# Mixture-of-experts stage of a fused decoder layer: routing inside the output projection, experts ordered by their token count, tokens held stationary

## The chip, the cores and the metric

One core of one Trainium2 chip runs the whole layer as one program. The metric is the device time of one execution in microseconds; the kernel before takes 1448.4 us (median of 3 runs, 1447.89 to 1451.6). All data are float32.

Five engines run their own instruction streams and meet at semaphores: TensorE (PE; its weight loads are shown as PEld), VectorE (DVE), ScalarE (ACT), GpSimd (POOL) and SyncE (SP). SP issues direct transfers on one queue, POOL issues direct and indirect (gather and scatter) transfers on another. 16 DMA engines serve both.

## The reference, cut to what matters

1056 tokens (1024 of a prompt, 32 of decoding) of 1024 features go through one layer: token mixers, an output projection `w_out` with a residual, a mixture of experts, and a gated embedding at the end. The mixture is what the change is about:

```
m        = rms_norm(h, g_ffn)                                # 1056 x 1024
g_sel    = argmax of m @ w_router_group                      # 1 of 4 groups
top_i    = top 2 of (m @ w_router_expert) in that group      # 2 of its 8 experts
w_k      = softmax(top 2 values) * softmax(group logits)[g_sel]
for each of the token's two experts e (32 experts in all):
    hidden = silu(m @ w_gate[e]) * (m @ w_up[e])             # 1024 -> 256, twice
    out   += w_k * (hidden @ w_down[e])                      # 256 -> 1024
h        = h + out
```

Each expert has 3 MB of weights, 32 experts 100.7 MB. There are 2112 (token, expert) pairs, 66 an expert on average. Worked out with the reference on its own inputs, the counts of the 32 experts run from 32 to 122. Experts 0 to 3 have 88, 60, 55 and 73 tokens. The other 28 sorted are 122, 111, 106, 89, 85, 83, 78, 75, 74, 74, 71, 67, 63, 61, 60, 59, 57, 56, 55, 53, 51, 47, 46, 45, 43, 37, 36, 32.

## The kernel before, in words

The program is written engine by engine (raw streams, no scheduler); the order of the code in each engine's block is the order on the engine, and each PE, ACT, DVE or DMA step counts up a semaphore that others wait for. Only the stages from the output projection on matter here.

*Output projection* (from `step_e` on each engine). For each of 9 tiles of 128 tokens (the last has 32), PE multiplies the attention half and the convolution half by `w_out` (`out_part`, L1710, for the last tile L1700). Between them it transposes the normalised row `m` of the tile before (`router`, L1726), and after them computes that tile's 36 router logits (`logits`, L1737). DVE adds the residual (L1209, L1215), makes `m` (`make_m`, L1226) and copies the logits (`take_logits`, L1232). POOL stores `m` to `m_dram` (L626). SP loads expert 0's weights before this stage.

*Routing* (DVE from L1265, PE L1760 and L1761, POOL L640 and L644). After the last logits DVE works out for all 9 tiles at once the group, the two experts, each token's rank within its expert (two matmuls with a matrix of ones and a triangular one give counts and ranks), and overflow blocks for experts with more than `CAP` = 128 tokens. POOL then writes each token's number into `list_dram` with 18 indirect transfers (2 choices x 9 tiles) and reads the lists back. SP loads experts 1 to 3 meanwhile.

*Experts* (`turn`, `block_act`, `take_rows`, `hidden`, `gather`, `scatter`). One block is one expert with up to 128 tokens; 32 blocks in the experts' own order. For a block POOL gathers up to 128 rows of `m_dram` into `xg` (L657), PE transposes them (`trans_rows`, L1769), DVE copies them out (L1357). PE multiplies with the gate and up weights as the stationary operand and 128 tokens as the moving one (`up`, L1778), which leaves `hidden` already transposed. ACT applies silu (L894), DVE multiplies (L1363). PE multiplies with `w_down` (`down`, L1788), ACT copies the result out (L898, L900) and POOL scatters the rows to `y_dram` (L669). PE's order in a steady block is `up(n)`, `trans_rows(n+1)`, `down(n-1)`. The weights sit in 4 slots; SP loads expert n+4 after `down(n)` (L491 to L493). 16 overflow blocks follow under an `If`.

*End*. SP loads `w_ple_gate`, `w_ple_proj` and the rows of `y_dram`; the two expert results are combined and the gated embedding is computed.

The lines that set the order in a steady block of PE and of POOL are these:

```
up(n, s % 2, s, i)
if not final:
    trans_rows(n + 1, 1 - s % 2, 2 * i + (s + 1) // 2)
if not begin:
    down(n - 1, 1 - s % 2, (s - 1) % 4)
...
gather(2 * i + 4 + u, u)
scatter(2 * i + u, u, i)
```

Of the kernel before, what the change touches and what calls it, by code (L numbers as in the profile page):

```python
# [80 lines left out]
def constants():  # L81
# [39 lines left out]
    c["c_blk"] = np.tile(np.arange(NOV, dtype=np.float32)[None, :], (P, 1))  # L121
# [33 lines left out]
KV_DONE = (32, 32, 0, 0, 0)  # L155

# [32 lines left out]
def _build(nc, I, O, ctx):  # L189
# [14 lines left out]
    list_dram = nc.dram_tensor("list_dram", [CAP * NBLK, 2], I32).ap()  # L204
# [16 lines left out]
    misc = sb("misc", 64)  # L221
# [67 lines left out]
    m_st = [view(R1, 12576 + 1024 * s, D) for s in range(2)]  # L289
    mT = [view(R1, 14624 + 1024 * s, DC, P) for s in range(2)]  # L290
    junkE = R1[:, 19744:19744 + 512].bitcast(BF16)
    h = view(R1, 0, TILES, D)

    scratch_at = [21504]

    def scratch(*dims):
        at = scratch_at[0]
        scratch_at[0] += int(np.prod(dims))
        assert scratch_at[0] <= 26880
        return view(R1, at, *dims)  # L300

    r_ms, r_h1, r_h2, r_t, r_tot, r_rank, r_a = (scratch(T, NE) for _ in range(7))
    r_cum = scratch(T + 1, NE)
    r_big = scratch(NE, NTH - 1)
    r_ov = scratch(4, NE)
    r_bb = scratch(NOV, NE)
    r_be = scratch(NOV)
    r_hg, r_hg2, r_ge = (scratch(T, GROUPS) for _ in range(3))
    r_c10 = scratch(T, NTH - 1)
    r_mg, r_ig, r_m1, r_i1, r_m2, r_i2, r_rk, r_bs, r_c, r_s, r_z, r_x, r_gw, r_e2 = (scratch(T) for _ in range(14))  # L310
    pos_i = sb("pos_i", 2 * TILES, I32)
    code = sb("code", 4 * TILES, I32)
    blk = sb("blk", NOV)
    ov_e = sb("ov_e", NOV, I32)
    small_i = sb("small_i", 4, I32)
    lg = sb("lg", TILES * RG)[:, :].rearrange("p (t c) -> p t c", t=TILES)

    SLOTS = [R4[:, 0:6144], R2[:, 0:6144], R1[:, 9216:15360], R1[:, 15360:21504]]
    wg = [s[:, 0:2048].rearrange("p (c f) -> p c f", c=DC) for s in SLOTS]
    wu = [s[:, 2048:4096].rearrange("p (c f) -> p c f", c=DC) for s in SLOTS]  # L320
# [51 lines left out]
    def _(sp):  # L372
# [27 lines left out]
        sp.dma_start(blk[:, :], I["c_blk"]).then_inc(S("code_in"), 16)  # L400
        sp.wait_ge(S("relbd_zero"), 1)
# [100 lines left out]
        load_expert(0, 0)  # L502
        over_tiles(sp, lambda prev, cur, nxt: load_x2(nxt) if nxt is not None else None)


        sp.wait_ge(S("logits_done"), TILES)
        sp.wait_ge(S("out0"), 32 * USES[0])
        sp.wait_ge(S("out1"), 32 * USES[1])
        for s in range(1, 4):
            load_expert(s, s)  # L510
        with sp.Fori(0, NE // 4 - 1) as i:
            for s in range(4):
                sp.wait_ge(S("y_full"), 8 * i + 2 * s + 2)
                load_expert(4 * i + 4 + s, s)
# [5 lines left out]
        sp.wait_ge(S("y_full"), 2 * NE)  # L520
        over = sp.value_load(small_i[0:1, 0:1], min_val=0, max_val=NOV)
        with sp.If(over > 0):
            for s in range(4):
                load_expert(sp.value_load(ov_e[0:1, s:s + 1], min_val=0, max_val=NE - 1), s)
            with sp.Fori(1, NOV // 4) as i:
                for s in range(4):
                    sp.wait_ge(S("y_full"), 2 * NE + 8 * i + 2 * s - 6)
                    load_expert(sp.value_load(ov_e[0:1, bass.ds(4 * i + s, 1)], min_val=0, max_val=NE - 1), s)
# [1391 lines left out]
```

## Time and profile before

| | |
|---|---|
| median of 3 runs | 1448.4 us |
| the profiled execution: its own time / span | 1454.46 / 1452.4 us |
| mean granted TensorE clock | 0.931 of full speed |
| PE / DVE / ACT / POOL busy | 87 / 28 / 22 / 12 % of the span |
| chain that ended last | PE 81 %, DMA 6 %, DVE 6 % |
| output projection (PE's first matmul to the last logits) | 675 to 818.6 us |
| routing (last logits to the first `up`) | 818.6 to 880.3 us |
| experts (first `up` to the end of the last `down`) | 880.3 to 1263.1 us |
| end | 1263.1 to 1452.4 us |

Durations below are of the profiled execution, 6.1 us above the median. A fully busy PE in a window does not say how fast it is, since matmuls overlap: a float32 matmul is two instructions, and the time from one group of them to the next is what counts. The four stage borders are from the timeline and from the chain of waits.

### The profile page before, as it was taken

The page shows a single profiled execution, that of the slowest core. Times are in us where ns is not written, and L with a number is a line of the kernel's source. Part 1 is how long each engine was busy: PE and PEld are TensorE (multiplying, and loading weights), DVE is VectorE, ACT ScalarE, POOL GpSimd, SP SyncE. Part 2 cuts the span into 40 slices and gives each one's busy share as a digit, 9 for nine tenths or more (in the row PEclk, how much of TensorE's full clock was granted, in tenths as well). Part 3 has the DMA queues.
Part 4 walks back from the last instruction along what each step waited for, and adds up shares of the span by engine and source line. Part 5 has one row for each costly group of instructions (what it writes and reads, how often), then busy time and mean ns, then how long its engine had stood idle before and what let it go on. Part 6 is the DMA issues. An engine that isn't in the chain of part 4 may idle for free.

```text
span 1452.4 us, 16889 instructions
## 1 busy us (share of the span) xinstructions
PE 1262.4 (87%) x6484; PEld 816.4 (56%) x6484; DVE 403.7 (28%) x829; ACT 320.8 (22%) x625; POOL 168.5 (12%) x222
## 2 busy tenths in 40 slices
PE   4999999999978887567999407999999999789995
PEld 1444445666555557243555307888888888534442
DVE  1121221122257775121322531111111111033332
ACT  2132321000057664130111200111111111123332
POOL 0000000000031221000000052222222221100000
PEclk9999999999979998787999758999999999979998
DMA  7111400130040005898111422888888888432210
GB/s 260 36 51 43 119 15 19 44 102 0 27 127 31 30 1 162 202 267 301 73 73 47 191 89 64 308 308 294 310 297 322 317 318 327 189 129 90 86 50 33
DMA packets 64453, 208.84 MB, mean 144 GB/s; under 512 B 16158, under 2 KB 29758, under 8 KB 48528
## 3 DMA queue, kind: packets, MB, share of 16 engines
q1 hardware_dynamic: 50704, 177.61, 35.6%
q0 software_dynamic: 13696, 30.49, 5.8%
q8 instruction: 37, 0.61, 0.2%
q14 instruction: 16, 0.13, 0.0%
HBM read 194.43 MB, written 29.89 MB: 154 GB/s over the span
## 4 chain that ended last, share of the span: by engine, by line
PE 81%; DMA 6%; DVE 6%; issue 3%; ACT 2%; POOL 1%; SPq 1%; POOLq 0%; ACTq 0%; DVEq 0%
PE pair L1778 17%; PE pair L1473 12%; PE pair L1525 11%; PE pair L1710 8%; PE pair L1877 8%; PE pair L1788 8%; DMA R<-in_cache_v 4%; PE pair L1552 3%; PE pair L1566 2%; PE pair L1769 2%; PE pair L1859 2%; PE pair L1579 2%; DVE R L1101 1%; PE pair L1603 1%; POOL list_dram L640 1%
## 5 line engine op out<-in xcount | busy, mean ns | idle before, releaser
L1778 PEld LDWEIGHTS pair<-R 128*128 128x128 f32 x2048 | 247.6, 197 | 16.5 <-issue 14.2
L1778 PE MATMUL pair<-R 128*128 128x128 f32 x2048 | 247.9, 282 | 1.7 <-DVE R L1357 1.7
L1525 PE MATMUL pair<-R 128*128 128x352 f32 x576 | 172.5, 463 | 0.4 <-ACT kts L758 0.4
L1473 PE MATMUL pair<-R 128*128 128x512 f32 x384 | 170.6, 601 | 0.8 <-DVE R L993 0.8
L1525 PEld LDWEIGHTS pair<-R 128*128 128x128 f32 x576 | 110.2, 192 | 61.8 <-issue 1.4
L1473 PEld LDWEIGHTS pair<-R 128*128 128x128 f32 x384 | 72.9, 193 | 87.8 <-issue 86.6
L1788 PE MATMUL pair<-R,bias_s 128*128 128x512 f32 x256 | 115.3, 593 | 1.4 <-DVE bias_s L1363 1.4
L1710 PE MATMUL pair<-R 128*128 128x512 f32 x256 | 114.6, 602 | 0.0
L1877 PE MATMUL pair<-R 128*128 128x512 f32 x256 | 112.9, 599 | 0.8 <-ACT R L932 0.8
L1357 DVE COPY R<-pair 128x512 f32<-128x512 f32 x64 | 41.3, 686 | 238.2 <-PE pair L1769 238.2
L1877 PEld LDWEIGHTS pair<-R 128*128 128x128 f32 x256 | 49.2, 193 | 62.9 <-issue 62.9
L898 ACT ACTIVATE R<-pair 128x512 f32<-128x512 f32 x32 | 19.1, 597 | 292.4 <-PE pair L1788 292.4
L1710 PEld LDWEIGHTS pair<-R 128*128 128x128 f32 x256 | 48.3, 193 | 55.6 <-issue 55.6
L1769 PE MATMUL pair<-ident,R 128*128 128x128 f32 x256 | 34.3, 278 | 45.8 <-DMA R<-m_dram,idx_c 45.8
L1788 PEld LDWEIGHTS pair<-R,bias_s 128*128 128x128 f32 x256 | 46.2, 190 | 48.2 <-issue 45.9
L1566 PE MATMUL pair<-ident,R 128*128 128x128 f32 x288 | 46.3, 302 | 22.1 <-DVE R L1101 16.2
L1769 PEld LDWEIGHTS pair<-ident,R 128*128 128x128 f32 x256 | 31.5, 189 | 46.6 <-issue 46.6
L1566 PEld LDWEIGHTS pair<-ident,R 128*128 128x128 f32 x288 | 34.0, 151 | 40.6 <-DVE R L1101 36.2
L807 ACT ACTIVATE R<-pair 128x512 f32<-128x512 f32 (+3 forms) x96 | 43.8, 484 | 43.3 <-PE pair L1566 43.0
L796 ACT ACTIVATE R<-R,small 128x1024 f32<-128x1024 f32 (+7 forms) x64 | 49.4, 772 | 6.0 <-DVE small L1092 5.5
L1092 DVE CUSTOM_DVE_ANT_0 R<-pair,R 128x1024 f32<-128x1024 f32 (+7 forms) x64 | 45.8, 753 | 13.8 <-PE pair L1552 13.7
L1552 PE MATMUL pair<-R 64*128 64x512 f32 (+3 forms) x192 | 44.6, 573 | 4.1 <-DVE small L1092 3.5
(266 smaller groups left out, 1172.0 us busy)
## 6 DMA issues: line engine op xcount, KB each, us to landing
R<-in_w_gate SPq DMA_DIRECT2D x32, 1024.0 KB, 7.3
R<-in_w_up SPq DMA_DIRECT2D x32, 1024.0 KB, 9.7
R<-in_w_down SPq DMA_DIRECT2D x32, 1024.0 KB, 12.9
R<-in_x_prompt SPq DMA_DIRECT2D x16, 512.0 KB, 3.5
R<-in_cache_k SPq DMA_DIRECT2D x8, 1024.0 KB, 7.8
R<-in_cache_v SPq DMA_DIRECT2D x8, 1024.0 KB, 19.7
R<-y_dram SPq DMA_DIRECT2D x16, 512.0 KB, 4.3
R<-in_w_in SPq DMA_DIRECT2D x3, 2048.0 KB, 10.3
```

The costliest lines, as they stand in the source:

```text
L796: act.activation(E[n % 2][hh][:, 0:w], E[n % 2][hh][:, 0:w], ACT.Exp, bias=nmax[:, k:k + 1], scale=-1.0, accum_out=den[:, k:k + 1]).then_i ...
L807: act.activation(PTb[n % 2][hh][:, j0:j0 + m, :], bk[4 + use % 2].rearrange("p (a b) -> p a b", b=P)[:, 0:m, ::-1], ACT.Copy).then_inc(S(" ...
L1092: dve.tensor_tensor_reduce(E[n % 2][hh][:, 0:w], bank[hh][:, 0:w], Z[2 * (pair % 2) + hh][:, SEQ - w:SEQ], -1.0, 3e38, ALU.add, ALU.min, n ...
L1473: last = mm(bk[4 + part][0:n, :], xTs[a.u][:, c, 0:n], wA[:, c, AD * part:AD * part + AD], start=(c == 0), stop=(c == DC - 1))
L1525: last = mm(bk[b][:, 0:n], wB[q % 2][:, c, which, :], xT[:, c, lo:lo + n], start=(c == 0), stop=(c == DC - 1))
L1552: last = mm(bank[hh][:, c0:c0 + m], QT[half, pair, P * i:P * i + P], KT[half, pair, c0:c0 + m], start=True, stop=True)
L1566: last = pe.transpose(bk[4 + use % 2][:, P * j:P * j + P], E[n % 2][hh][:, P * (j0 + j):P * (j0 + j) + P], ident[:, :])
L1710: last = mm(bk[2 * pair + j][0:n, :], lhs[:, q, P * a.t:P * a.t + P], w_out[:, c0 + q, 512 * j:512 * j + 512], start=(q == 0), stop=(q == ...
L1769: last = pe.transpose(bk[j][:, CAP * (c % 4):CAP * (c % 4) + CAP], xg[u][:, c:D:DC], ident[0:CAP, 0:CAP])
L1778: last = mm(bk[2 + u][:, CAP * (2 * side + j):CAP * (2 * side + j) + CAP], w[:, c, j:FE:2], xgT[u][:, c, :], start=(c == 0), stop=(c == DC ...
L1788: last = mm(bk[4 + 2 * u + j][0:CAP, :], hT[u][:, q, :], wd[s][:, q, 512 * j:512 * j + 512], start=(q == 0), stop=(q == 1))
L1877: last = mm(bk[2 + j][0:n, :], hnT[a.u][:, c, 0:n], w_pg[c][:, 512 * j:512 * j + 512], start=(c == 0), stop=(c == DC - 1))
```

## The change

1. *Routing tile by tile.* The group, the experts and the ranks are worked out for one tile in the steps of the output projection (`choose`, `place` on DVE, `rank` on PE, `enlist` on POOL) with a running count `r_cum`. The lists in `list_dram` are now one stretch of 1152 entries an expert.
2. *Order.* When all counts are known DVE ranks experts 4 to 31 by count. Experts 0 to 3 come first in fixed order. Then `PLAN` sets 18 "F" blocks (one expert, up to 128 tokens) for the largest and 5 "P" blocks (two experts, up to 64 tokens each) for the 10 smallest. That makes 27 blocks for 32 experts. SP reads each expert's number from `order_i`. The token lists are fetched by an indirect transfer for each block (`fetch`), five blocks ahead.
3. *Tokens stationary.* `up` now holds 128 tokens (or 64 and 64) as the stationary operand and streams 512 columns of gate and up weights: 8 float32 matmuls of 512 columns in place of 32 of 128. `hidden` then comes out with tokens on partitions, and two PE transposes and an ACT copy a block turn it (`trans_hidden`, `keep_hT`). In a P block each matmul is two, on 64 partitions of the output each.
4. *Order in a block.* PE: `up(n)`, `down(n-1)`, `trans_rows(n+1)`, `trans_hidden(n)`. POOL: `fetch(n+5)`, `gather(n+2)`, `scatter(n)`. `down` has one pair of PSUM banks in place of two.
5. *Weights.* Experts 0 and 1 are loaded before the output projection, 2 at its end, 3 after the last logits. Gate and up are loaded when `up` of the slot's last block is done, `w_down` when its `down` is.
6. *Overflow.* Up to 24 further blocks under an `If`, planned on DVE during block 2 (`spill_blocks`). The weights `w12` are worked out during block 0.

```
+NSTAT = 4
+PLAN = "FFPFFFFPFFFPFFFFPFFFPFF"
...
-            for j in range(2):
-                for c in range(DC):
-                        last = mm(bk[2 + u][:, CAP * (2 * side + j):CAP * (2 * side + j) + CAP], w[:, c, j:FE:2], xgT[u][:, c, :],
...
+            wide = CAP // len(parts)
+            for c in range(DC):
+                for k, (s, _) in enumerate(parts):
+                    r = slice(wide * k, wide * k + wide)
+                    last = mm(bk[2 + u][r, :].rearrange("p (w f) -> p w f", w=2), xgT[u][:, c, r], wgu[s][:, :, c, :],
+                              start=(c == 0), stop=(c == DC - 1))
             last.then_inc(S("gu_full"), 1)
...
+        def trans_hidden(n, u):
             pe.wait_ge(S("hidden"), n + 1)
+            if not (isinstance(n, int) and n < 1):
+                pe.wait_ge(S("hT_done"), n)
+            for q in range(2):
+                last = pe.transpose(bk[7][:, FE * u + P * q:FE * u + P * q + P], sg[u][:, q:FE:2], ident[:, :])
+            last.then_inc(S("hT_full"), 1)
...
+        trans_rows(0, 0, 16)
+        for n in range(NBM):
+            up(n, n % 2, members(n))
+            if n >= 1:
+                down(n - 1, (n - 1) % 2, members(n - 1))
+            if n + 1 < NBM:
+                trans_rows(n + 1, (n + 1) % 2, 16 * uses_of(n + 1))
+            trans_hidden(n, n % 2)
+        down(NBM - 1, (NBM - 1) % 2, members(NBM - 1))
...
+        def rank(a):
+            n, t, u = a.rows, a.t, a.u
+            pe.wait_ge(S("chosen"), t + 1)
...
+            last = mm(bk[4][0:n, 0:NE], tri[0:n, 0:n], r_a[u][0:n, :], start=True, stop=(t == 0))
+            if t >= 1:
+                last = mm(bk[4][0:n, 0:NE], ones[:, 0:n], r_cum[1 - u], start=False, stop=True)
...
+        for t in range(TILES):
+            residual_att(fixed(t))
+            if t >= 2:
+                place(fixed(t - 2))
+            residual_conv(fixed(t))
+            make_m(fixed(t))
+            if t >= 1:
+                choose(fixed(t - 1))
+        place(fixed(TILES - 2))
+        choose(fixed(TILES - 1))
+        place(fixed(TILES - 1))
...
+        for n in range(NBM):
+            if n + NSTAT + 1 < NBM:
+                fetch(n + NSTAT + 1)
+            if n + 2 < NBM:
+                pool.wait_ge(S("lists_in"), 16 * max(1, n + 4 - NSTAT))
+                gather(n + 2, n % 2, lists[0:CAP, 2 * n + 4:2 * n + 5])
+            scatter(n, n % 2, lists[0:CAP, 2 * n + 1:2 * n + 2])
...
+        for l in range(NSTAT, NE):
+            e = sp.value_load(order_i[0:1, LOADS[l][1]:LOADS[l][1] + 1], min_val=0, max_val=NE - 1)
+            sp.wait_ge(S("gu_full"), LBEFORE[l] + 1)
+            load_wide(e, LSLOT[l])
+            sp.wait_ge(S("y_full"), 2 * LBEFORE[l] + 2)
+            load_down(e, LSLOT[l])
```

PE at the start of the expert stage, in the kernel before: L1760 and L1761 are the two routing matmuls, L1769 `trans_rows`, L1778 `up`, L1788 `down`.

```order
L1760 MATMUL pair<-R,ones 128x288
L1761 MATMUL pair<-R,tri 128x288
L1769 MATMUL pair<-ident,R 128x128 x8
L1778 MATMUL pair<-R 128x128 x32
L1769 MATMUL pair<-ident,R 128x128 x8
L1778 MATMUL pair<-R 128x128 x32
L1769 MATMUL pair<-ident,R 128x128 x8
L1788 MATMUL pair<-R,bias_s 128x512 x4
```

The same place after the change (and on to the second `down`); L1893 is the last `rank`, L1915 the counts, L1925 `trans_rows`, L1939 `up`, L1948 `trans_hidden`, L1962 `down`.

```order
L1893 MATMUL pair<-R,ones 32x32
L1915 MATMUL pair<-R,ones 128x32
L1925 MATMUL pair<-ident,R 128x128 x8
L1939 MATMUL pair<-R 128x512 x8
L1925 MATMUL pair<-ident,R 128x128 x8
L1948 MATMUL pair<-ident,R 128x128 x2
L1939 MATMUL pair<-R 128x512 x8
L1962 MATMUL pair<-R,bias_s 128x512 x4
L1925 MATMUL pair<-ident,R 128x128 x8
L1948 MATMUL pair<-ident,R 128x128 x2
L1939 MATMUL pair<-R 128x512 x8
L1962 MATMUL pair<-R,bias_s 128x512 x4
```

`down` has moved in front of `trans_rows`, so that between `trans_rows` and the next `up` there stand now two transposes in place of a whole `down`.

POOL in a steady block of the kernel before (L654 and L665 copy a column of indices, L657 gathers four blocks ahead, L669 scatters):

```order
L654 COPY idx_c<-lists 128x1
L657 DMA R<-m_dram,idx_c 128x1024
L665 COPY idx_c<-lists 128x1
L669 DMA y_dram<-R,idx_c 2112x1024
L654 COPY idx_c<-lists 128x1
L657 DMA R<-m_dram,idx_c 128x1024
```

The same engine after the change, from the reading of the first lists on (L738; L748 `fetch`, L757 `gather`, L765 `scatter`):

```order
L738 DMA lists<-list_dram 128x4x2
L757 DMA R<-m_dram,lists 128x1024 x2
L748 DMA lists<-list_dram,idx_i 128x2 x2
L757 DMA R<-m_dram,lists 128x1024
L765 DMA y_dram<-R,lists 2112x1024
L748 DMA lists<-list_dram,idx_i 128x2
L757 DMA R<-m_dram,lists 128x1024
L765 DMA y_dram<-R,lists 2112x1024
```

A gather now stands behind the scatter of the block three before it, for two blocks ahead, with a fetch between them.

## Rows read from the trace of the kernel before

**Rows 1.** Chain of waits from the lists on: start us, length us, what.
```profile
870.00 2.04 DMA lists<-list_dram
873.23 4.18 DMA R<-m_dram,idx_c
...
880.27 9.28 PE pair L1778 x64
...
1021.93 7.53 PE pair L1778 x64
1030.34 3.44 PE pair L1788 x8
1033.77 7.53 PE pair L1778 x64
...
1259.37 3.71 PE pair L1788 x8
1264.59 7.06 DMA y_dram<-R,idx_c
```

**Rows 2.** Timeline, projection tile 5, last tile, last list write: start, length us, instruction.
```profile
754.55 1.87 PE L1737 MATMUL pair<-R 128*128 128x36 f32 x16
...
757.66 1.29 DVE L1226 SCALAR_TENSOR_TENSOR R<-R,small 128x1024 f32<-128x1024 f32 x1 [0.25 <-DVE small L1221]
...
814.62 1.27 DVE L1226 SCALAR_TENSOR_TENSOR R<-R,small 32x1024 f32<-32x1024 f32 x1
...
818.61 0.18 DVE L1232 COPY lg<-pair 32x36 f32<-32x36 f32 x1 [2.49 <-PE pair L1737]
...
867.76 0.88 POOL L640 DMA_INDIRECT list_dram<-code,pos_i  x1 [0.30 <-issue]
870.00 0.59 POOL L644 DMA_DIRECT2D lists<-list_dram  x1 [1.36 <-DMA list_dram<-code,pos_i]
```

**Rows 3.** Groups by line and shape, 805 to 900 us: busy us, mean ns | idle before.
```profile
L640 POOL DMA_INDIRECT list_dram<-code,pos_i x18 | 17.6, 978 | 32.5 <-DVE small_i L1341 27.3 <-issue 5.2
...
L1301 DVE TENSOR_TENSOR R<-R 128x32 f32<-128x32 f32 x9 | 1.7, 192 | 0.3
...
L1317 DVE TENSOR_TENSOR R<-R,blk 128x512 f32<-128x512 f32 x1 | 0.7, 693 | 0.0
```

**Rows 4.** Timeline of one steady block, same columns as rows 2.
```profile
1022.10 0.34 SPq L491 DMA_DIRECT2D R<-in_w_gate  x1
...
1023.49 1.02 POOL L669 DMA_INDIRECT y_dram<-R,idx_c  x1 [2.54 <-ACT R L900]
1029.29 1.05 PE L1769 MATMUL pair<-ident,R 128*128 128x128 f32 x8
1029.93 1.29 DVE L1357 COPY R<-pair 128x512 f32<-128x512 f32 x2 [6.64 <-PE pair L1769]
...
1030.17 3.60 PE L1788 MATMUL pair<-R,bias_s 128*128 128x512 f32 x8
...
1031.56 1.05 POOL L657 DMA_INDIRECT R<-m_dram,idx_c  x1 [0.87 <-POOL idx_c L654]
```

**Rows 5.** Chain of waits, first stage: full width, and three outputs of 32 partitions.
```profile
182.21 6.87 PE pair L1473 x16
...
212.62 7.04 PE pair L1463 x48
```

**Rows 6.** Transfers by line: count, KB each, median us from issue to landing.
```profile
R<-in_w_down SPq DMA_DIRECT2D x32, 1024.0 KB, 12.9
...
y_dram<-R,idx_c POOLq DMA_INDIRECT x32, 9.6
```

**Rows 7.** Windows: length, busy us of PE, PEld, DVE, ACT, POOL; clock, DMA share, GB/s.
```profile
835.00:840.00 5.00, 0.00 (x0) 0.00 (x0) 4.45 (x17) 0.00 (x0) 0.00 (x0) 0.50 1.02 421
...
1200.00:1250.00 50.00, 50.00 (x345) 42.37 (x343) 7.28 (x13) 6.39 (x14) 8.45 (x14) 1.00 0.86 324
...
1265.00:1266.00 1.00, 0.00 (x0) 0.00 (x0) 0.00 (x0) 0.00 (x0) 0.57 (x1) 0.95 0.48 131
1266.00:1267.00 1.00, 0.00 (x0) 0.00 (x0) 0.00 (x0) 0.00 (x0) 0.00 (x0) 0.50 0.99 238
```

More of the change, by code:

```diff
@@ L302, in _build, with scratch, take @@
[L302 to L310, printed above, removed]
+    def scratch(at, end):
+        place = [at]
+        def take(*dims):
+            start = place[0]
+            place[0] += int(np.prod(dims))
+            assert place[0] <= end
+            return view(R1, start, *dims)
+        return take
@@ L508, in _ @@
         sp.wait_ge(S("out1"), 32 * USES[1])
[L509 to L514, printed above, removed]
+        load_wide(3, LSLOT[3])
+        load_down(3, LSLOT[3])
+        sp.wait_ge(S("order_done"), 1)
+        for l in range(NSTAT, NE):
[4 more added lines that the diff above has]
+            load_down(e, LSLOT[l])
         sp.wait_ge(S("routed"), 1)
@@ L693, in _ @@
+            with pool.Fori(0, NOV // 2) as i:
+                for d in range(2):
+                    spilled(i, d)
         pool.end_ifs()
@@ new lines, in place @@
+        def place(a):
+            n, t, u = a.rows, a.t, a.u
+            dve.wait_ge(S("rank_full"), t + 1)
+            then(dve.tensor_tensor(r_rb[0:n, :], bk[4][0:n, 0:NE], base[0:n, :], ALU.add))
+            for k in range(2):
+                then(dve.tensor_tensor(r_prod[0:n, :], r_h[u][k][0:n, :], r_rb[0:n, :], ALU.mult))
+                then(dve.tensor_reduce(r_posf[0:n, k:k + 1], r_prod[0:n, :], AX.X, ALU.add))
+            dve.tensor_copy(pos_i[0:n, 2 * t:2 * t + 2], r_posf[0:n, :]).then_inc(S("pos_done"), 1)
@@ new lines, in _ @@
+        then(dve.tensor_reduce(r_ee[:, NSTAT:NE], r_gt, AX.X, ALU.add))
+        dve.tensor_copy(order_i[:, :], r_ee[:, NSTAT:NE]).then_inc(S("order_done"), 1)
+        then(dve.tensor_scalar(r_bb, r_ee, float(LROWS), None, ALU.mult))
+        for half in range(2):
+            rows = slice(64 * half, 64 * half + 64)
+            then(dve.tensor_copy(r_pb[rows, :], r_bb[rows, NFULL + half:NE:2]))
+        then(dve.tensor_scalar(idx_i[:, NSTAT:NFULL], r_bb[:, NSTAT:NFULL], part, None, ALU.add))
@@ L1377, in _ @@
+        take_rows(0, 0)
+        for n in range(NBM):
+            hidden(n, n % 2)
+            if n + 1 < NBM:
+                take_rows(n + 1, (n + 1) % 2)
+            if n == 0:
+                weigh_experts()
+            if n == 2:
+                spill_blocks()
+                dve.wait_ge(S("routed"), 1)
         over = dve.value_load(small_i[0:1, 0:1], min_val=0, max_val=NOV)
         with dve.If(over > 0):
-            experts(NE, NOV)
+            with dve.Fori(0, NOV // 2) as i:
+                for d in range(2):
+                    n, u = NBM + 2 * i + d, (NBM + d) % 2
+                    take_rows(n, u)
+                    hidden(n, u)
```

627 lines of the change are left out of this document (348 added, 279 removed).

## The prediction

> **What bounds the kernel now.** I read the chain of waits first. PE carries 81 % of it. In the expert stage it holds PE alone: `up` 7.53 us, `down` 3.44 us and the transposes, one block every 11.84 us (1021.93 to 1033.77) [rows 1]. From the last logits (818.8) to the first `up` (880.27) PE is idle but for two matmuls, and the chain goes through DVE, the 18 list writes, the list read and the first gather [rows 1 to 3]. The reader is to see there a serial stretch of 61 us. The timeline of one block [rows 4] shows what stands behind what within 11.84 us. Last, the transfers: an expert's last piece lands 12.9 us after its issue, a scatter 9.6 us after its own [rows 6], and the DMA engines are busy 0.86 of the time at 324 GB/s, against 421 GB/s when weights alone move [rows 7]. So PE is the bound, with DMA close behind.
>
> The sum is made against the profiled execution: 1454.5 us, of which 880.3 lie ahead of the first `up`, 382.8 in the expert stage (to 1263.1, [rows 1]) and 191.4 after it. It is 6.1 us above the median, and I take that off at the end.
>
> **Routing.** Gone is the whole stretch from 818.8 on. New on DVE are 17 small instructions a tile in `choose` and 6 in `place`. Nine of 128x32 take 1.7 us and 0.3 us between them [rows 3], so 0.22 each: 3.8 and 1.3 us. In the middle tiles they hide. `choose` starts when `make_m` ends (758.95), 4.4 us after PE has gone over to the logits (754.55) [rows 2], and ends at 8.2, while PE's next `rank` stands at 9.4 (16 narrow matmuls 1.7, 16 of 512 columns 6.9, transposes 0.9). If that cover of 1.2 us is gone, its excess comes 7 times. At the end nothing hides them. `choose(6)` and `place(6)` push the last `m` from 815.9 [rows 2] to 819.8; then `choose(7)` (to 823.6), `rank` and `place(7)` (825.4), `choose(8)` (829.4), `rank` and `place(8)` (831.3) follow in series. `rank` on PE is up to four instructions; sixteen narrow ones take 1.87 us [rows 2], so 0.43 us each and 2.8 us over the stage: 834.1. POOL issues two list writes of 1.3 us (17.6 us for 18 with 0.3 between, [rows 3]); the last is issued at 835.4 and lands 2.2 later (867.76 to 870.00, [rows 1, 2]); the list read takes 2.0 and the gather 4.2 [rows 1], the transposes and copies before `up` 2.7: 846.7. Expert 3's 3 MB are issued at about 828 and lie under the list writes. Their cost is between 0 and 7.5 us (3.15 MB at 421 GB/s, [rows 7]); I take 3.5, since only the second half overlaps. First `up` at 850, against 880.3: **-30 us**. The sorting of the experts by count on DVE (7 instructions of 128x784, about 1.0 us each by L1317's 0.69 for 512, [rows 3]) ends about when the first gather lands and costs nothing; if it were late, some 2 us.
>
> Moved at no cost: expert 1's load before the projection (3.15 MB at 421 GB/s are 7.5 us, by which the rows of tile 1 behind it land later; they are wanted only when the attention half of tile 1 is done, three groups of 16 matmuls or 20.6 us after PE's start), the larger blank list at the start, the weights `w12`, ACT's copies (2 us of a block).
>
> **PE's work in the expert stage.** `up` is 16 instructions of 512 columns in place of 64 of 128: 6.87 us [rows 5] in place of 7.53. `down` stays 3.44. The gap between `down` and the next `up` grows. It holds `trans_rows`, after whose first half (0.64 us) DVE needs 1.29 us for two copies [rows 4], plus 0.05: 1.98 us. `trans_hidden` fits under it. Before, `down` hid the copies and the gap was 0.88 (1029.29 to 1030.17). So a block takes 12.29 us against 11.84, but there are 27 and not 32. The stage: 27 x (6.87 + 3.44) + 26 x 1.98 = 329.9, plus 1.75 for the first `up` at the half clock (9.28 less 7.53, [rows 1]), 1.4 before the last `down`, 1 for changes between widths: 334. `spill_blocks` is 38 DVE instructions, 8 of them of 768 elements, some 13.5 us in front of `hidden(3)`; PE wants that after 11.2: +3. Together 337, against 382.8: **-46 us**.
>
> This holds only if the two halves of a P block run side by side. The trace has no two outputs of 64 partitions, but 48 instructions on three outputs of 32 take 7.04 us where 16 of full width take 6.87 [rows 5], so three ran at once. Bounds: nothing, or 5 x 10.3 = 51.6 us if they are serial. I take the row.
>
> **What the transfers give back.** Two waits are new.
>
> First, POOL's order. A gather is issued behind the scatter and a fetch (1.3 us each), and `scatter(n-1)` waits for ACT's copy: it is issued 1.56 us after the end of `down(n-1)` (1021.93 to 1023.49, [rows 1, 4]). PE wants the gathered rows one block after that `down`. So a block is at least 1.56 + 2.6 + the gather's landing. Idle queues give 4.2 for it [rows 1]: 8.4 us, hidden under 12.29. But the weights are issued at the same `down` (1022.10, the scatter at 1023.49, [rows 4]), and under them a scatter takes 9.6 [rows 6]. With that the block is 13.8, 1.5 above PE's, or +36 us over 24 blocks. These are the ends, 0 and 36. I go by the loaded row, the nearer in kind, less 0.4, since the gather is issued 2.6 us further into the weights' 12.9 than that row's scatter: 13.4, **+27 us**. Before, the gather was issued 21 us ahead of its use (1031.56 against 1029.29 + 2 x 11.84, [rows 4]) and nobody waited. Queued behind the waiting scatter are now the fetch and that gather; PE waits for the gather.
>
> Second, P blocks need 6.3 MB. An expert with its rows costs the engines 0.86 x 11.84 = 10.2 us [rows 7]; 28 of them after the start are 285 us, below 337, so DMA is not the bound on average. But a P block needs 20.4 us of it in 12.3. The 3 or 4 blocks between two of them save 2.1 each, about 7.4 of the 8.1 wanted, and slots come free late. I take 1.4 for each of 5: **+7 us** (bounds 0 and 30).
>
> **The end.** `w_ple_proj` is now loaded a block earlier and no longer under the last scatter (7.06, [rows 1]); I give it 4: **-3 us**.
>
> Sum: 850 + (337 + 27 + 7) + 191.4 - 3 = 1409.4, less 6.1: **1403 us**.
>
> The Trainium skill, DMA: Bandwidth & Descriptors, section Queues, rings and completion order, says that an engine takes turns between queues by whole packets of some 9 to 17 descriptors. This speaks against the change: three POOL transfers in a row could each wait for such a packet of weight rows. By that rule (8 KB at 421/16 GB/s is 0.31 us, so 2.8 to 5.3 us a turn) the chain from the scatter to the gathered rows is an estimated 11 to 18 us and a block 12 to 19, which is the third rival's ground. The 9.6 us of a scatter under load do not refute it.
>
> **Rivals.**
> 1. *The row transfers stay hidden.* For it: they are small, and the weight queue is idle part of each block (0.86). Against: 9.6 us. Stage 339, first `up` at 847: 847 + 339 + 188.4 - 6.1 = 1368 us. Chance 22 %.
> 2. *P blocks are serial.* For it: no such pair in the trace. Against: rows 5. 51.6 us more, some 8 of them in place of waits: 1447 us. Chance 8 %.
> 3. *Slower: the gather waits for the scatter's landing.* 1.56 + 9.6 + 4.2 = 15.4 us a block, of which PE works 10.3. That is the point from which it decides: at 15.4 the stage (416) eats what routing and end save. But in such an idle stretch the clock falls: after PE's last matmul at 1263.1 it is 0.95 over the third microsecond and 0.50 (1.2 GHz against 2.4) then [rows 7], and a start at that level costs 1.75 more [rows 1]. 26 x 17.1 + 15 = 460 us for the stage: 850 + 460 + 188.4 - 6.1 = 1492 us. Against: DMA engines have room, and a gather needn't wait for a landing. Chance 6 %.
> 4. *The change doesn't do what it says:* an overflow block runs. All 24 would, serially, well over 20 us each. The counts exclude it (the largest is 122 of 128, the largest in a pair 55 of 64). Chance 1 %.
>
> **How the numbers follow.** The forecast has 63 %, its own range is 1378 to 1424 (the two waits, 34 us in the sum, between 9 and 55). The range for 8 in 10 reaches down to the first rival and towards the second: 1364 to 1440. About 0.3 % (4 us) is what can be told from no change. Faster holds the forecast and the rivals 1 and most of 2: 0.91; same 0.02; slower 0.07.
>
> **What would show it.** Right: first `up` at 845 to 855; `up` 6.9 us, also in P blocks; 1.9 to 2.0 us between `down` and `up` with DVE's copies as releaser; PE waiting at `trans_rows` for the gather, 0.7 to 1.5 us in most blocks; the last `down` ending near 1221. Wrong: a P block's `up` of 13.7 us (rival 2), clock below 1 in the expert stage (rival 3), PE waiting for weights rather than rows for more than 15 us, or `rank` waiting for `choose` in every tile.

## The result and the profile after

The changed kernel takes 1400.4 us (median of 4 runs, 1392.4 to 1402.8) against 1448.4: ratio 0.966, 95 % interval 0.9638 to 0.9682. The forecast was 1403. The profiled execution took 1402.83 us (span 1401.0).

| stage of the profiled executions | before | after | forecast |
|---|---|---|---|
| start to the first projection matmul | 675.1 | 669.3 | 669 (the 6.1 us taken off at the end) |
| from there to the first `up` | 205.2 | 176.8 | 174.9 |
| experts: first `up` to the end of the last `down` | 382.8 | 368.8 | 371 |
| from there to the end of the execution | 191.4 | 187.9 | 188.4 |

The first row lies ahead of what the change is about. In the twelve kernels of the experiments it reads 664.1 to 668.9 and only in the kernel before 675: its profiled execution was 6.1 us above its median, and one transfer of `cache_v` on its chain took 28.87 us against 24.24. Without that row the profiled executions differ by 45.9 us (28.4 + 14.0 + 3.5), the medians by 48.0. What the routing and the faster `up` gave is read from the two traces; no run undoes either alone. The chain of waits from the last list write on, which answers to [rows 1] (start us, length us, what):

```profile
826.83 1.94 DVE R L1385
...
831.79 1.38 POOL list_dram L724
833.48 1.95 DMA list_dram<-code,pos_i
835.71 2.37 DMA lists<-list_dram
839.08 4.14 DMA R<-m_dram,lists
843.36 1.96 PE pair L1925 x8
846.09 9.68 PE pair L1939 x16
...
1211.20 3.71 PE pair L1962 x8
1216.43 3.20 DMA y_dram<-R,lists
```

The list write, the list read and the gather take what they took before [rows 1] to within 0.4 us, 34 us earlier. Expert 3's 3 MB, issued from 823.9 on, are through at about 833.0, ahead of the last list write (833.48). Windows of that stretch, as in [rows 7] (us, busy us of PE, PEld, DVE, ACT, POOL, granted clock, DMA share, GB/s):

```profile
828.00:834.00 6.00, 1.12 (x6) 0.86 (x6) 5.30 (x17) 1.62 (x3) 2.63 (x3) 0.50 0.83 345
834.00:836.00 2.00, 0.00 (x0) 0.00 (x0) 1.90 (x4) 0.00 (x0) 0.65 (x2) 0.50 0.01 0
```

From 833.0 to 833.5 the DMA share is 0.05, so the last list write did not lie beside the weights: this run does not show what they would cost it. The last scatter takes 3.2 us in place of 7.06.

Two steady blocks, in PE's timeline. L1925 is `trans_rows`, L1939 `up`, L1962 `down`; the bracket is the idle time in front and what ended it.

```profile
982.02 7.13 PE L1939 MATMUL pair<-R 128*128 128x512 f32 x16 [0.77 <-DVE R L1455]
988.99 3.60 PE L1962 MATMUL pair<-R,bias_s 128*128 128x512 f32 x8
994.16 1.15 PE L1925 MATMUL pair<-ident,R 128*128 128x128 f32 x8 [1.58 <-DMA R<-m_dram,lists]
...
996.32 7.09 PE L1939 MATMUL pair<-R 128*64 128x512 f32 x32 [0.78 <-DVE R L1455]
1003.34 3.70 PE L1962 MATMUL pair<-R,bias_s 128*128 128x512 f32 x8
1006.88 1.04 PE L1925 MATMUL pair<-ident,R 128*128 128x128 f32 x8
...
1008.93 2.41 PE L1939 MATMUL pair<-R 128*128 128x512 f32 x5 [0.78 <-DVE R L1455]
```

The P block's `up` (x32, starting at 996.32) takes 7.09 us, an F block's 7.13: the halves run side by side. PE waits 1.58 us for the gathered rows in the first block and not at all in the second. POOL over the same stretch (L765 scatter, L748 fetch, L757 gather):

```profile
981.70 1.00 POOL L765 DMA_INDIRECT y_dram<-R,lists  x1 [13.08 <-ACT R L1017]
983.01 1.02 POOL L748 DMA_INDIRECT lists<-list_dram,idx_i  x1 [0.30 <-issue]
984.34 0.99 POOL L757 DMA_INDIRECT R<-m_dram,lists  x1 [0.31 <-issue]
```

The gather is issued 2.64 us behind the scatter (1.31 and 1.33 for the two steps). All of PE's waits from 846 to 1215 us (us in total, times, the longest), and the gathers' landing in the steady blocks:

```profile
PE pair L1939 <- DVE R L1455: 19.9, 27, 0.8
PE pair L1925 <- DMA R<-m_dram,lists: 15.4, 13, 3.1
PE pair L1948 <- DVE R L1460: 1.8, 1, 1.8
PE pair L1962 <- ACT bias_s L1009: 0.7, 1, 0.7
```
```profile
DMA to landing us min/median/max: 8.3/9.8/11.6
```

### The profile page after: what moved, and what is told of

It is laid out like the page before. It is cut to its first block, busy times and chain, and to the rows that moved or that the text cites. A ratio compares the mean times of both kernels' runs of the same rounds, so it can differ in the third digit from the quotient of the medians.

```text
span 1401.0 us, 13600 instructions
## 1 busy us (share of the span) xinstructions
PE 1215.4 (87%) x4994; PEld 651.9 (47%) x4994; DVE 431.5 (31%) x972; ACT 326.2 (23%) x637; POOL 169.5 (12%) x171
## 4 chain that ended last, share of the span: by engine, by line
PE 71%; DMA 12%; DVE 8%; issue 4%; ACT 3%; POOL 1%; SPq 1%; POOLq 0%; DVEq 0%; ACTq 0%
PE pair L1618 12%; PE pair L1670 12%; PE pair L1939 9%; PE pair L1855 8%; PE pair L2042 8%; DMA R<-m_dram,lists 7%; PE pair L1962 4%; DMA R<-in_cache_v 3%; PE pair L1697 3%; PE pair L1711 2%; PE pair L2024 2%; PE pair L1724 2%; DVE R L1455 2%; DVE R L1229 1%; PE pair L1748 1%
## 5 line engine op out<-in xcount | busy, mean ns | idle before, releaser
L1939 PE MATMUL pair<-R 128*128 128x512 f32 (+1 forms) x512 | 201.3, 617 | 19.9 <-DVE R L1455 19.9
L1670 PEld LDWEIGHTS pair<-R 128*128 128x128 f32 x576 | 110.2, 192 | 61.8 <-issue 1.5
L1939 PEld LDWEIGHTS pair<-R 128*128 128x128 f32 (+1 forms) x512 | 79.6, 180 | 124.8 <-issue 99.1
L1618 PEld LDWEIGHTS pair<-R 128*128 128x128 f32 x384 | 72.9, 193 | 87.5 <-issue 86.3
L1962 PE MATMUL pair<-R,bias_s 128*128 128x512 f32 (+1 forms) x256 | 98.0, 597 | 0.7 <-ACT bias_s L1009 0.7
L2042 PEld LDWEIGHTS pair<-R 128*128 128x128 f32 x256 | 49.7, 194 | 63.7 <-issue 63.7
L1460 DVE TENSOR_TENSOR R<-pair,R 128x256 f32<-128x256 f32 x27 | 11.5, 425 | 206.6 <-ACT R L1005 206.5
L1855 PEld LDWEIGHTS pair<-R 128*128 128x128 f32 x256 | 48.4, 194 | 55.9 <-issue 55.9
L1455 DVE COPY R<-pair 128x512 f32<-128x512 f32 x54 | 35.0, 686 | 100.3 <-PE pair L1925 100.1
L1711 PE MATMUL pair<-ident,R 128*128 128x128 f32 x288 | 45.0, 296 | 23.0 <-DVE R L1229 17.1
L1962 PEld LDWEIGHTS pair<-R,bias_s 128*128 128x128 f32 (+1 forms) x256 | 38.3, 173 | 56.5 <-issue 55.6
L1005 ACT ACTIVATE R<-pair 128x256 f32<-128x256 f32 x27 | 10.3, 383 | 223.7 <-PE pair L1939 223.7
L765 POOL DMA_INDIRECT y_dram<-R,lists x27 | 27.1, 1005 | 283.9 <-ACT R L1017 263.3
L1925 PE MATMUL pair<-ident,R 128*128 128x128 f32 x216 | 31.9, 293 | 28.7 <-DMA R<-m_dram,lists 28.6
L1711 PEld LDWEIGHTS pair<-ident,R 128*128 128x128 f32 x288 | 32.9, 148 | 41.4 <-DVE R L1229 36.9
```

What stands on the lines that cost most here:

```text
L1455: dve.tensor_copy(xgT[u][:, 4 * j:4 * j + 4, :], bk[j][:, 0:4 * CAP].rearrange("p (g n) -> p g n", g=4)).then_inc(S("rowsT_done"), 1)
L1618: last = mm(bk[4 + part][0:n, :], xTs[a.u][:, c, 0:n], wA[:, c, AD * part:AD * part + AD], start=(c == 0), stop=(c == DC - 1))
L1670: last = mm(bk[b][:, 0:n], wB[q % 2][:, c, which, :], xT[:, c, lo:lo + n], start=(c == 0), stop=(c == DC - 1))
L1711: last = pe.transpose(bk[4 + use % 2][:, P * j:P * j + P], E[n % 2][hh][:, P * (j0 + j):P * (j0 + j) + P], ident[:, :])
L1855: last = mm(bk[2 * pair + j][0:n, :], lhs[:, q, P * a.t:P * a.t + P], w_out[:, c0 + q, 512 * j:512 * j + 512], start=(q == 0), stop=(q == ...
L1939: last = mm(bk[2 + u][r, :].rearrange("p (w f) -> p w f", w=2), xgT[u][:, c, r], wgu[s][:, :, c, :], start=(c == 0), stop=(c == DC - 1))
```

## The experiments

A block is measured from one `up`'s start to the next. Without any wait it is 12.46 us in the changed kernel. "The stage" is the expert stage of the one profiled execution, from the first `up` to the end of the last `down`: 368.8 us in the changed kernel. Unless said otherwise an edit is made to the changed kernel alone.

### The gather 1.33 us earlier

```
+gather(n + 2, ...)
 fetch(n + NSTAT + 1)
-gather(n + 2, ...)
 scatter(n, ...)
```

> POOL issues gather(n+2) ahead of fetch(n+5), so each gather is issued 1.33 us earlier after the scatter; nothing else is changed. Theory A (the chain down, scatter, fetch, gather, trans_rows sets the block where PE waits): the waits after down, 18.2 us in 14 blocks, shrink by up to 1.33 us each to about 5 us, and the slow clock behind them with them: 12 to 17 us less, 1383 to 1388 us, ratio to the kernel before 0.956. Theory B (the gather's rows come when the weights in flight are through, whatever the moment of issue): landings grow by 1.3 us and the time stays at 1398 to 1402 us.

Measured: 1395.7 us, ratio 0.9636 (0.9591 to 0.9681), which can't be told from 0.966 (0.9638 to 0.9682). The stage was 368.0 us (368.8 before the edit), PE's waits for rows 14.1 us. (In the changed kernel these are 15.4 us in 13 blocks; the 18.2 us in 14 that the expectation starts from are not waits for rows alone.)

```profile
PE pair L1925 <- DMA R<-m_dram,lists: 14.1, 11, 2.4
```
```profile
DMA to landing us min/median/max: 9.5/10.5/12.0
```

Theory B holds in the main: issued 1.33 us earlier, the gather took longer by 0.7 (median) to 1.2 us (minimum), and the waits fell by 1.3 us in sum, where theory A wanted them at about 5. The time is 2 us below B's range.

### The gather a whole block earlier

```
-if n + 2 < NBM: gather(n + 2, n % 2, ...)
+if n + 3 < NBM: gather(n + 3, (n + 1) % 2, ...)      # gather(2) goes ahead of the loop
```

> POOL gathers one block further ahead (gather(n+3) behind scatter(n-1) in place of gather(n+2)); the fetched lists are counted on two semaphores. Theory A: PE waits for no gather any more; the 18.2 us of waits and most of the 6.4 us of slow clock behind them go: stage 368.8 to 343 us, 1374 us, ratio 0.949. Theory C (the DMA engines set the pace, and the row waits only show it): PE waits for weights in place of rows, the waits stay above 12 us in sum, time 1388 us or more.

Measured: 1379.8 us, ratio 0.9524 (0.948 to 0.9569), stage 345.7 us. In PE's waits from 846 to 1192 us no transfer is left but one of the end:

```profile
PE pair L1945 <- DVE R L1461: 20.5, 27, 0.8
PE pair L1954 <- DVE R L1466: 2.7, 1, 2.7
PE pair L2002 <- DMA R<-in_p_prompt: 0.9, 1, 0.9
PE pair L1968 <- ACT bias_s L1015: 0.7, 1, 0.7
```

Theory A holds and C falls: the landings are still 8.4 to 11.2 us, nobody waits for them, and the weights come in time behind P blocks too. The row waits, with what they brought in slow clock and slow starts, were worth 23.1 us of the stage (25.8 were expected). The only slow `up`s left are the first and the one behind `spill_blocks`; the two blocks of a pair (its `up`, then its `down`) are 12.61 and 12.81 us here.

### trans_rows before down again

On top of the last edit:

```
 up(n, n % 2, members(n))
+trans_rows(n + 1, ...)
 down(n - 1, ...)
-trans_rows(n + 1, ...)
 trans_hidden(n, n % 2)
```

> As the kernel with gathers a block further ahead, and PE's order in a block is that of the kernel before: up(n), trans_rows(n+1), down(n-1), trans_hidden(n). DVE's two copies then lie under down. Theory A: the gap of 2.0 us between down's end and the next up falls to about 0.45, with 0.9 between up and down: a block of 11.75 in place of 12.46 us, 18 us less than with the gathers ahead alone: 1356 us, ratio 0.936. Theory C (DMA is next): a stage of 326 us asks for more than the engines give around P blocks; PE waits for weights 10 us or more and the time is 1365 to 1372 us.

Measured: 1352.05 us, ratio 0.9327 (0.9288 to 0.9367), stage 322.4 us. The clean block is 11.43 us in place of 12.46. PE's waits for `w_up` are 2.3 us, once. This edit alone gave 23.3 us of the stage, more than the 18 expected.

### One pair in place of five

```
-PLAN = "FFPFFFFPFFFPFFFFPFFFPFF"
+PLAN = "F" * 26 + "P"
```

> One P block in place of five, 31 blocks in place of 27 (the two smallest experts alone are paired); all else as the changed kernel. Theory A (a P block costs PE what an F block costs, and some waits): 4 blocks more of 12.5 us and about 0.5 us of row wait, less 5 us of waits that P blocks bring: 47 us more, 1447 us, ratio 1.0. Theory D (pairs give back as weight waits most of what they save): 1410 to 1425 us.

Measured: 1440.4 us, ratio 0.9953 (0.9932 to 0.9974), stage 405.5 us for 31 blocks. The four pairs are worth 36.7 us of the stage, where four clean blocks are 49.8: about a quarter is given back, by row waits (6.5 us with one pair, 15.4 with five), the slow clock behind them and the 0.5 us that a pair is longer. It lies between the two theories, nearer A.

### The gather behind the scatter's landing

```
 pool.wait_ge(S("lists_in"), ...)
+if n >= 1:
+    pool.wait_ge(S(f"rows_out{(n - 1) % 2}"), 16 * ((n - 1) // 2 + 1))
 gather(n + 2, ...)
```

> The changed kernel, with POOL waiting for the scatter of block n-1 to land before it issues gather(n+2). It puts the third rival into effect. Expected by the rival's price: a block of 1.56 + 8.9 + the gather's landing. If the gather then finds idle queues (4.2 us) the block is about 15 to 16 us, and with cold starts (up 8.8 to 9.1 us) up to 17: stage 400 to 450 us, 1440 to 1480 us. If the gather's landing stays 9 us under weights, the block is over 19 us: stage 500 us, above 1530 us.

Measured (one run): 1466.9 us, beside 1449.4 for the kernel before; stage 435.1 us. The gather's median landing is 4.3 us, and PE's timeline shows long and short blocks in turn:

```profile
990.55 3.60 PE L1964 MATMUL pair<-R,bias_s 128*128 128x512 f32 x8
1000.30 1.97 PE L1927 MATMUL pair<-ident,R 128*128 128x128 f32 x8 [6.16 <-DMA R<-m_dram,lists]
...
1003.06 9.02 PE L1941 MATMUL pair<-R 128*128 128x512 f32 x16 [0.36 <-DVE R L1457]
1011.91 3.60 PE L1964 MATMUL pair<-R,bias_s 128*128 128x512 f32 x8
1015.35 1.05 PE L1927 MATMUL pair<-ident,R 128*128 128x128 f32 x8
```

After 6.16 us of waiting `up` starts at the half clock (9.02 us), and the next `trans_rows` waits for nothing. PE's waits for rows are 61.8 us, again in 13 of 26 blocks. The third rival's mechanism, had it been there, would indeed have made the kernel slower than before.

### The two halves one after the other

```
-for c in range(DC):
-    for k, (s, _) in enumerate(parts):
+for k, (s, _) in enumerate(parts):
+    for c in range(DC):
```

> In a P block's up the eight matmuls of the first expert come first, then the eight of the second, in place of alternating; down is unchanged. Theory E (two halves run side by side only when their instructions alternate): up of a P block takes 13.7 in place of 7.1 us, five times: stage about 33 us longer less a few us of waits that are hidden, 1425 to 1432 us. Rival (the halves overlap anyway, or the order within PE's queue doesn't matter): up of a P block stays at 7.1 us and the time at 1396 to 1403 us.

Measured (one run): 1420.0 us, stage 390.5 us. Each of the five P blocks has this `up`:

```profile
922.89 12.29 PE L1939 MATMUL pair<-R 128*64 128x512 f32 x32 [0.78 <-DVE R L1455]
```

12.29 us, not 7.1 and not quite 13.7: theory E in its direction (1425 to 1432 us expected). Here the two outputs of 64 partitions run at once when their instructions alternate, and overlap little when they do not. `down`, whose pairs alternate too, was left as it was.

### Less weight in flight, twice

From the fifth expert on 0.9 of an expert's 3 MB isn't loaded, once by partitions and once by columns (gate and `w_down` are loaded whole). Both kernels leave out part of the mixture's work and are there for their times alone.

```
-load_wide(e, LSLOT[l])
+dma_start(SLOTS[s][0:16, 2048:4096], wu_r[e][0:16])            # the first
+dma_start(SLOTS[s][:, 2048:2048 + 256], wu_r[e][:, 0:256])     # the second
```

> The changed kernel, but from the fifth expert on only 16 of the 128 partitions of w_up are loaded (0.9 MB of an expert's 3 left out), so the weights in flight behind down are less by 30 %. Theory B (the gather lands when the weights in flight are through): the gather's median landing falls from 9.4 to about 7 us, PE's waits for it from 15.4 to under 2 us, the stage from 368.8 to about 346 us, as with the gather ahead. Theory A' (the gather takes about as long under any weight transfers, since the two queues take turns): landing stays above 9 us and the waits above 10 us.

> From the fifth expert on only 256 of the 2048 columns of w_up are loaded, over all 128 partitions (0.9 MB of 3 left out), where the run with 16 of 128 partitions had one 128 KB transfer that took 9.2 us. Theory B: median landing of the gather falls to about 7 us and the waits for it to under 2 us behind F and P blocks alike, stage about 346 us. Theory F (the waits of about 6 us behind P blocks in that run come from the two experts' weights ahead of the gather, not from the uneven transfer): waits of more than 3 us remain behind each P block.

The first (1405.7 us, stage 374.3) is muddled by the form of its short load: the 128 KB went to 16 partitions. That load itself has a median landing of 9.2 us, against 8.9 for the 128 KB over all partitions in the second, which explains little, and the cause of the following stays open. Its `trans_rows` waited at six places behind the first, 21.2 us in sum, four of them 4.2 to 5.6 us, in the second block behind a P block; a gather took up to 14.0 us. The second (1389.6 us, stage 356.5; one run each) has a median landing of 7.9 us. Its landings and all its waits for rows after the first gather:

```profile
DMA to landing us min/median/max: 6.4/7.9/11.8
```
```profile
964.43 1.97 PE L1925 MATMUL pair<-ident,R 128*128 128x128 f32 x8 [3.71 <-DMA R<-m_dram,lists]
...
1031.17 1.15 PE L1925 MATMUL pair<-ident,R 128*128 128x128 f32 x8 [1.43 <-DMA R<-m_dram,lists]
...
1057.07 1.17 PE L1925 MATMUL pair<-ident,R 128*128 128x128 f32 x8 [0.55 <-DMA R<-m_dram,lists]
...
1083.26 1.16 PE L1925 MATMUL pair<-ident,R 128*128 128x128 f32 x8 [0.66 <-DMA R<-m_dram,lists]
...
1146.69 1.16 PE L1925 MATMUL pair<-ident,R 128*128 128x128 f32 x8 [0.15 <-DMA R<-m_dram,lists]
...
1184.94 1.15 PE L1925 MATMUL pair<-ident,R 128*128 128x128 f32 x8 [0.31 <-DMA R<-m_dram,lists]
```

6.8 us in place of 15.4. What remains lies in a P block or in the two behind it, where two experts' weights are issued within 4 us. Theory B holds for F blocks; of P blocks F is right, in a weaker form.

### Gate and up issued before w_down

```
 load_wide(e, LSLOT[l])                               # waits for up
-sp.wait_ge(S("y_full"), 2 * LBEFORE[l] + 2)
-load_down(e, LSLOT[l])
+sp.wait_ge(S("y_full"), 2 * LBEFORE[l - 1] + 2)      # w_down of the load before
+load_down(e_prev, LSLOT[l - 1])
```

> The changed kernel with SP's order alone altered: gate and up of load l+1 are issued ahead of w_down of load l, that is right after up(n) and no longer after down(n-1). The 2 MB start some 3.5 to 4.5 us earlier in the block; POOL's order stays. Theory B (the gather lands when the weights in flight are through): the gather, issued 4.2 us after down, finds most of them landed; its median landing falls from 9.4 to 6 us or less, the waits for it from 15.4 to under 4 us, stage 368.8 to 347 us, 1378 us. Theory A' (a gather takes 9 us beside any weights, as e7 may be read): landing stays at 9, waits stay at 12 us or more, time 1395 to 1402 us.

Measured: 1393.0 us, ratio 0.9613 (0.9563 to 0.9663), stage 360.8 us. POOL's order is untouched, and yet the gather's landing has a median of 7.6 us, with these waits:

```profile
DMA to landing us min/median/max: 5.3/7.6/11.8
```
```profile
PE pair L1929 <- DMA R<-m_dram,lists: 10.3, 7, 2.3
```

Again F blocks wait no more and the rest lies behind P blocks, where two experts' weights are issued close together (behind the first pair 5 MB from 930.7 to 936.5 us, the gather at 938.4). A third of the expected gain came. The interval overlaps the changed kernel's (0.9638 to 0.9682), so the gain in time is not clear of noise; the landings and the waits are what speaks.

### Eight pairs

On top of gathers ahead and `trans_rows` first, 24 blocks: `PLAN = "FPFPFFPFPFFPFPFFPFPF"`.

> Gathers a block further ahead and trans_rows before down, as before, and 8 P blocks (the 16 smallest experts, 32 to 63 tokens) in place of 5: 24 blocks in place of 27. Theory A (PE is the bound): 3 blocks of 11.6 us less and 3 to 8 us of waits for weights more: stage 322.4 to 293 us, 1323 us, ratio 0.914. Theory C (DMA becomes the bound: 88 MB of weights and 25 MB of rows at 421 GB/s are 268 us, but slots come free late around P blocks): stage 305 to 322 us, 1335 to 1352 us.

Measured: 1347.7 us, ratio 0.931 (0.9286 to 0.9333), stage 313.5 us. Three blocks fewer gave 9 us of stage and 4 of time (the intervals overlap); PE now waits for `w_up`, at 7 places (us in total, times, the longest):

```profile
PE pair L1945 <- DMA R<-in_w_up: 18.4, 7, 4.1
```

Theory C.

### All together, and one step too far

The four edits that helped (gathers a block ahead, `trans_rows` first, gate and up before `w_down`, eight pairs), the two memsets of `xg` moved behind the list read, and `spill_blocks` cut into 8 parts over 8 blocks:

```
 PLAN = "FPFPFFPFPFFPFPFFPFPF"; gather(n + 3); trans_rows before down; load_wide(l + 1) before load_down(l)
 pool.dma_start(lists[...], list_dram[...])
+pool.memset(xg[0], 0.0); pool.memset(xg[1], 0.0)
-if n == 2: spill_blocks()
+if n >= 2 and spill_parts is not None: next(spill_parts, "end")
```

> All together: gathers a block further ahead, trans_rows before down, 8 P blocks, gate and up ahead of w_down on SP, the two memsets of POOL moved behind the list read, spill_blocks in 8 parts over 8 blocks. Theory A: against the run with 8 pairs (1347.7 us, 18.4 us of waits for w_up, 13.14 us at the block with spill_blocks) 1.7 us come from the memsets, 1.6 from spill_blocks, 12 to 20 from w_up with the slow clock behind it: 1325 to 1332 us, ratio 0.917. Theory C (DMA is the bound with 8 pairs, whatever the order of issue): the waits for w_up stay above 12 us, 1338 to 1346 us.

Measured: 1333.5 us, ratio 0.9197 (0.9154 to 0.924): the fastest version. Stage 300.9 us; `spill_blocks` costs nothing now (its blocks are 11.4 to 11.9 us, where it was one of 13.14). The waits for `w_up` that remain stand between the two theories; they and the windows:

```profile
PE pair L1958 <- DMA R<-in_w_up: 9.9, 3, 3.6
```
```profile
900.00:970.00 70.00, 70.00 (x269) 31.01 (x268) 17.29 (x34) 10.97 (x24) 18.16 (x18) 1.00 0.99 392
970.00:1035.00 65.00, 61.38 (x219) 27.12 (x218) 8.10 (x15) 9.38 (x21) 15.13 (x15) 0.95 1.01 415
```

The DMA engines are busy all the time (share 0.99 and 1.01; 0.93 and 0.97 with five pairs, gathers ahead and `trans_rows` first). PE is busy 94 to 100 % there as well, so the two are close, and I take it, without a run for it, that a better order of issue has little left to move.

The last run puts expert 3's load behind the list read and splits the memsets (`sp.wait_ge(S("lists_in"), 16)` ahead of `load_wide(3, ...)`).

> The kernel with all edits together, with two changes at the end of the routing: expert 3's 3 MB are issued when the first lists are read and no longer 8 us ahead of the last list write, and POOL's two memsets stand one behind the last list write and one behind the issue of the list read. From PE's first projection matmul to the first up it is 176.8 us in the changed kernel and 176.0 with all edits (the last write, the list read and the gather took 2.6, 3.6 and 5.0 us there against 2.2, 3.4 and 4.1 in the changed kernel). Theory G (expert 3's load in flight costs those 1.5 us, the memset that POOL's gather waited for 0.3 more): 174.2 us, and 1331 to 1332 us in all. Rival H (DVE's wide operations beside POOL's issue of transfers make them longer, not the load): 175.7 to 176.2 us and 1333 to 1334 us.

Measured: 1338.0 us, ratio 0.9234 (0.9207 to 0.9261), 4 us slower by the medians; the intervals overlap, but the stretch up to the first `up` is 4.4 us longer in the profile. Its chain:

```profile
830.41 1.94 DMA list_dram<-code,pos_i
832.35 0.28 issue
832.63 2.46 DMA lists<-list_dram
...
836.09 9.16 DMA R<-m_dram,lists
```

The 3 MB were issued at 835.2 to 836.0, the gather at 836.1, and it took 9.16 us in place of 4.98 (4.14 in the changed kernel). From the first projection matmul to the first `up` it is 180.4 us (176.0 with all edits). Both theories missed: the last list write, now with no weights beside it, took 1.94 us in place of 2.32, and the load fell on the gather. This gather's landing under one expert's weights is like the 9 us and more of the steady blocks.

## Why the prediction was right, point by point

- *Routing, -30 us: right.* 176.8 us against 174.9, by two misses of opposite sign. Contention from expert 3 was put at 3.5 us (0 to 7.5) and was nothing: the load was through at 833.0 and the last list write came behind it, since it was itself late. (With all edits together that write did lie beside the end of the load and took 2.32 us in place of 1.95.) Counted from the first projection matmul the last list write was issued 3.8 us later than worked out. 1.7 of these are a DVE instruction of 0.24 us that took 1.93 (826.83) beside POOL's two memsets (826.85 to 828.7), the rest are small terms of the serial chain. From that write to the first `up` it was 12.6 us, where 2.2 + 2.0 + 4.2 + 2.7 had been counted; 1.0 of the 1.5 more is POOL's time from the landed list to the gather's issue (838.08 to 839.08); [rows 1] show the same 1.2 us before (872.04 to 873.23), and the sum left it out. A middle tile is 16.85 us where it was 16.41: `rank`'s 0.43 us, as said, and `rank` waits for `choose` only in the last three places.
- *PE's work: near, small terms off, all one way.* The clean block is 12.46 us, not 12.29 (`up` to `down` 6.98 in place of 6.87), +4 us over the stage; a pair's two blocks are 0.5 us longer together, +2.5; the cold first `up` 9.67 us, +1. `spill_blocks` took 1.8 us of waiting and a slow `up` behind it (8.77), 3.4 us against 3. The stage without row waits (the gathers a block ahead) is 345.7 us where 337 was taken: 8.7 us too few.
- *Rows, 27 + 7 = 34 us: the mechanism right, the loop wrong.* The gather landed in 9.8 us, where 9.2 was taken, and by "a block is at least" 1.56 + 2.6 + 9.8 each block would have been 14.0 us, 38 us over the stage. The waits were 15.4 us, 13 of 26 blocks. This is the step that failed, though the time came out: the scatter goes when `down(n-1)` is done, and PE's wait at `trans_rows` comes behind that `down`. So the wait of one block is slack for the next, and waits come roughly in turns, as at 994.16 and 1006.88, worth about half on average. A term I left out here and had only in the third rival came on top: 6.4 us of slow clock. By my own list a clock below 1 in the stage would have shown that rival; it came without it (0.97 over the stage). Behind the 3.05 us wait that ended at 1035.5 the granted clock went from 1.00 to 0.50 (1.2 GHz), and `up` took 9.14 us; four `up`s of the stage besides the first were slow. The windows over it, columns as above:

```profile
1032.00:1034.00 2.00, 0.48 (x2) 0.00 (x0) 0.00 (x0) 0.60 (x1) 0.00 (x0) 1.00 1.02 424
1034.00:1036.00 2.00, 0.46 (x2) 0.47 (x3) 0.00 (x0) 0.00 (x0) 1.65 (x2) 0.89 1.01 428
1036.00:1038.00 2.00, 1.94 (x10) 1.53 (x8) 1.15 (x2) 0.03 (x1) 1.38 (x2) 0.50 1.01 385
```

  The waits and three of the four slow `up`s (4.8 us; the fourth is `spill_blocks`' and stays) are 20.2 us; moving the gather away gave back 23.1, the rest being slower transposes and starts behind the waits. Not every wait brought the slow clock: behind 1.55 us (1091.22) it was 0.50 from 1094 to 1096 and `up` took 8.83 us, behind 1.58 us (994.16) it stayed at 1.00 and `up` took 7.09. What decides between the two is not shown. P blocks gave no weight waits at all (0 us, bounds 0 and 30 right, 7 taken): their 6.3 MB delayed rows, not themselves.

  So the stage came near its forecast (368.8 against 371) partly by luck: what the transfers gave back was 23.1 us and not 34, PE's own work 345.7 and not 337, and the two misses cancel to 2 us.
- *What sets a gather's 9 us* wasn't asked. The experiments answer it: hardly POOL's place (1.33 us earlier took 1.3 us off the waits), but the weights in flight. With gate and up started earlier or cut, the landing falls to 7.6 and 7.9; behind the scatter's landing it is 4.3; with 3 MB issued a moment before it, 9.2. In these runs the landing goes with the weights that are still in flight. One run does not fit: with the same 0.9 MB cut by partitions the median was 8.3 us and the longest 14.0. How the engines choose between the queues is not shown.
- *The end, -3: right* (-3.5; the scatter 3.2 us where 4 was given).
- *Rivals.* The first (transfers hidden, 1368) was tried as gathers ahead: 1380. The second (serial P blocks, +52 in the stage) was tried for `up` alone, which costs +21.7 (5 x 5.2 less some waits); its other half, a serial `down`, was not tried. The third came to 1467, not 1492, through the same turn-taking of waits: its mean block was 16.1 us, its price had 17.1.

By the Trainium skill's rule on queues (DMA: Bandwidth & Descriptors, Queues, rings and completion order), the chain from the scatter's issue to the gathered rows was estimated at 11 to 18 us. It measured 2.64 + 9.8 = 12.4 us, so the trace agrees, at the lower end. It is weak support: with the gather ahead of the fetch there was one turn less, worth 2.8 to 5.3 us by that estimate, and the chain went only from 12.4 to 1.31 + 10.5 = 11.8 us.

## What to carry to other kernels

Before a transfer is put behind a wait, ask what else is issued at that same moment: a small gather beside 3 MB of weights lands late with them, and a microsecond of earlier issue buys little, while a whole block of lead buys all of it. When you price a wait in a loop, find out whether the wait itself lies inside the loop that closes it; if not, it can come every second time and count half (here 13 of 26 blocks, in two kernels), plus the slow clock behind some of them. A gap on the bound engine (here 1 us a block for two DVE copies) can be filled by the order of its own instructions: that was worth 23.3 us of the stage, as much as all the waits.

## What the runs showed of the hardware that I had not expected

- Two matmuls on 64 partitions of the output each overlap fully when their instructions alternate (7.09 us for 32 instructions, 7.13 for 16 of full width) and little when one expert's come first and then the other's (12.29 us).
- The same 128 KB a load cost more to 16 partitions than to 128 (one run each): gathers beside them landed after up to 14.0 us against 11.8, and PE's waits were 21.2 us against 6.8.
- POOL's memsets stop some small DVE instructions. L1385 over all nine tiles (ns min/median/max):

```profile
L1385 DVE TENSOR_SCALAR R<-misc,R x9: 241/241/1926, 707.2 to 826.8; 128x32 f32<-128x32 f32 x8, 32x32 f32<-32x32 f32 x1
```

The 1926 ns stand beside two POOL memsets (826.85 to 828.7). With the memsets moved it took 0.23 us, and the same memsets now lay beside two others: a cast and a tensor_scalar took 2.05 and 1.98. A reduction of 128x784 that lay beside a memset in the last run (833.33) stayed at 0.97 us. The Trainium skill, SBUF — State Buffer, Who interferes with whom, says that a cast, a copy or a tensor_scalar can share a port pair with GpSimd that one of the two locks for a whole instruction, and that a reduction never does; the trace agrees. Moving the memsets brought 0.8 us of the 1.7 (176.8 to 176.0 us from the first projection matmul to the first `up`). Of the rest some 0.3 went to POOL's first gather, which then waited for them; and the last list write (2.32 us against 1.95) and that gather (4.98 against 4.14) took longer in that run.
